# A hybrid encoder layer with 32 experts: token rows fetched as half rows to 128 partitions, and each expert's tokens dealt to slots four apart

## The reference

```python
grp_logits = xt @ w_grp + b_grp                      # 4 groups
g_sel = argmax(grp_logits);  p_g = softmax(grp_logits)[g_sel]
top_val, top_idx = top_k(e_logits[g_sel], 2)         # 2 of the 8 experts of that group
weights = p_g * softmax(top_val)
h = silu(xb @ w_e1[e]) * (xb @ w_e3[e])              # 1024 -> 512, for each token of expert e
y[token] += (h @ w_e2[e]) * weight                   # 512 -> 1024
```

## Time and profile before

| | us |
|---|---|
| median of 3 runs (1262.17 to 1263.38) | 1262.66 |
| the profiled execution, its own time | 1259.6 |
| its span, first to last instruction | 1257.9 |
| PE busy | 1103.4 (88%) |
| DVE busy | 434.3 (35%) |
| POOL busy | 384.7 (31%) |
| ACT busy | 356.3 (28%) |
| 96 weight loads of 2 MB, median issue to landing | 36.2 |
| DMA queue of the weights (q1), share of 16 engines | 51.8% |

### The profile page before, as it was taken

How to read it: one execution, slowest core, us unless ns; L and a number is a source line. 1 busy time by engine, 2 the same in 40 slices (tenths; PEclk the granted TensorE clock), 3 DMA queues, 4 the chain that set the end, 5 groups by cost and what they waited for, 6 DMA issues and landing times. The chain is left out here.

```text
span 1257.9 us, 20475 instructions
## 1 busy us (share of the span) xinstructions
PE 1103.4 (88%) x8243; PEld 841.1 (67%) x8243; DVE 434.3 (35%) x957; ACT 356.3 (28%) x749; POOL 384.7 (31%) x425
## 2 busy tenths in 40 slices
PE   5999899899999999998998978878888888777784
PEld 4998898899998878888996754444444444444342
DVE  6697633972111744432334432220101000000006
ACT  5547533452223645442334330000000000000000
POOL 4454468741223342333552011121221111111100
PEclk9999999989999989999998969989999999999998
DMA  7322336173325411116225939999999999999985
GB/s 126 88 81 68 77 88 168 45 196 98 93 53 180 142 34 51 52 43 214 80 72 174 429 122 407 404 406 400 404 406 408 405 406 415 404 402 404 405 373 226
DMA packets 149146, 284.58 MB, mean 226 GB/s; under 512 B 43988, under 2 KB 119348, under 8 KB 132688
## 3 DMA queue, kind: packets, MB, share of 16 engines
q1 hardware_dynamic: 93696, 244.94, 51.8%
q10 hardware_dynamic: 49632, 27.46, 8.1%
q0 software_dynamic: 5744, 11.15, 2.6%
HBM read 267.08 MB, written 24.31 MB: 232 GB/s over the span
## 5 line engine op out<-in xcount | busy, mean ns | idle before, releaser
L2528 PE MATMUL bank<-e_w,b_xT 128*64 128x256 f32 x2048 | 235.2, 387 | 37.0 <-DVE b_xT L2555 28.1
L489 PE MATMUL bank<-xhi,cv_w_hi 128*128 128x272 f32 x848 | 258.6, 305 | 8.4 <-PEq L133 2.6
L475 POOL TENSOR_TENSOR cv_w_lo<-cv_w_raw,cv_w_hi 128x1024 fp32r<-128x1024 f32 (+1 forms) x69 | 164.4, 2383 | 308.0 <-ACT cv_w_hi L468 291.5
L489 PE MATMUL bank<-xhi,cv_w_lo 128*128 128x272 f32 x848 | 249.3, 294 | 0.0
L489 PE MATMUL bank<-xlo,cv_w_hi 128*128 128x272 f32 x848 | 248.8, 293 | 0.0
L2528 PEld LDWEIGHTS bank<-e_w,b_xT 128*64 128x64 f32 x2048 | 145.9, 139 | 116.2 <-DVE b_xT L2555 33.5
L489 PEld LDWEIGHTS bank<-xhi,cv_w_hi 128*128 128x128 f32 x848 | 163.8, 193 | 17.1 <-issue 9.7
L489 PEld LDWEIGHTS bank<-xlo,cv_w_hi 128*128 128x128 f32 x848 | 164.6, 194 | 1.1
L489 PEld LDWEIGHTS bank<-xhi,cv_w_lo 128*128 128x128 f32 x848 | 164.1, 194 | 0.0
L2540 PE MATMUL bank<-e_w,b_hiddenT 128*64 128x512 f32 x512 | 124.9, 632 | 33.5 <-issue 18.3
L2496 POOL COPY b_target<-slot_target 128x1 int32 (+1 forms) x31 | 5.6, 181 | 358.4 <-ACT b_y L2550 358.4
(11 more groups left out here) (449 smaller groups left out, 1649.7 us busy)
## 6 DMA issues: line engine op xcount, KB each, us to landing
e_w<-in_w_e SPq DMA_DIRECT2D x96, 2048.0 KB, 36.2
cv_w_raw<-in_w_in ACTq DMA_DIRECT2D x34, 512.0 KB, 4.2
cv_w_raw<-in_w_in SPq DMA_DIRECT2D x18, 512.0 KB, 3.8
cv_w_raw<-in_w_br_b ACTq DMA_DIRECT2D x8, 512.0 KB, 4.2
o_raw<-in_w_out SPq DMA_DIRECT2D x16, 256.0 KB, 4.1
y_rows<-choice_rows SPq DMA_DIRECT2D x8, 512.0 KB, 6.8
g_values_gates<-g_z_stage ACTq DMA_DIRECT2D x12, 272.0 KB, 4.6
f_gates<-g_values_gates SPq DMA_DIRECT2D x2, 1088.0 KB, 8.7
```

The source lines that it names most:

```text
L475: self.k.nc.gpsimd.tensor_tensor(self.wlo[:, s, 0:nk, :], self.raw[:, s, 0:nk, :], self.whi[:, c % OPS, 0:nk, :].bitcast(F32), ALU.subtract)\
L489: last = self.k.nc.tensor.matmul(self.bank(c, h)[:, 0:HALF], w, x[:, d, cols], start=(d == 0 and n == 0), stop=(d == nk - 1 and n == 2))
L2528: last = nc.tensor.matmul(k.bank[bank][sl[a], 0:FH], xT[:, d, :], w[slot][:, d, FH * a:FH * a + FH], start=(d == 0), stop=(d == KD - 1))
```

## The change

Three things are changed, and small ones follow from them.

1. `b_rows` has 128 partitions of 512 floats: slot s has the first half of its token's row in partition s and the second half in partition 64+s. The gather reads half rows of 2 KB from a view of `token_rows` with two rows for a token; `token` numbers are doubled, and `k.half` adds 0 or 1 by partition half.
2. The turn takes the lower and the upper 64 partitions alternately, into banks 0 and 5; the gain is multiplied and copied in two instructions of 256 columns, and PE starts on the first four runs of channels after the first of them. `place_first` writes both halves of its product to one bank, and DVE adds them in one instruction.
3. Ranks are compared with `k.slots` in place of `k.iota`. It holds, in slot 4g+r, the number g+16r. So ranks 0 to 15 sit in slots 0, 4, 8, ..., ranks 16 to 31 in slots 1, 5, ..., and so on.

```diff
+SPREAD = SLOTS // 16
...
-    k.xg = k.over("b_rows", [SLOTS, RING, D], F32, "late", 3 * size)
+    k.xg = k.over("b_rows", [128, RING, D // 2], F32, "late", 3 * size)
+    k.halves = k.table.rearrange("t (two n) -> (t two) n", two=2)
...
+            g.iota(sN[:].rearrange("p (a g r) -> p a g r", a=2, r=SPREAD), pattern=[[0, 2], [1, SLOTS // SPREAD], [SLOTS // SPREAD, SPREAD]],
+                   base=0, channel_multiplier=0).then_inc(made, 1)
...
-                    last = V.tensor_scalar(r1[j][0:n, :], k.iota[0:n, :], k.rank[0:n, j, t:t + 1], None, ALU.is_equal)
+                    last = V.tensor_scalar(r1[j][0:n, :], k.slots[0:n, :], k.rank[0:n, j, t:t + 1], None, ALU.is_equal)
...
-            g.indirect_dma_start(out=xg[:, slot, :], out_offset=None, in_=k.table,
+            g.indirect_dma_start(out=xg[:, slot, :], out_offset=None, in_=k.halves,
...
-            nc.tensor.matmul(k.bank[0][:, 0:64], xg[:, slot, 0:128], k.ident[0:64, 0:64], start=True, stop=True)
-            for d in range(1, KD):
-                last = nc.tensor.transpose(k.bank[0][:, 64 * d:64 * d + 64], xg[:, slot, 128 * d:128 * d + 128],
-                                           k.ident[0:64, 0:64])
+            nc.tensor.matmul(X[0][:, 0:64], xg[lo, slot, 0:128], k.ident[lo, lo], start=True, stop=True)
+            nc.tensor.transpose(X[1][:, 0:64], xg[hi, slot, 0:128], k.ident[hi, hi])
+            for d in range(1, 4):
+                for a in range(2):
+                    last = nc.tensor.transpose(X[a][:, 64 * d:64 * d + 64], xg[sl[a], slot, 128 * d:128 * d + 128],
+                                               k.ident[sl[a], sl[a]])
...
-                nc.tensor.matmul(R[h][0:SLOTS, :], k.first_oh[:], k.xn[0:NS, 512 * h:512 * h + 512], start=True, stop=True)\
-                    .then_inc(placed, 1)
-            pe.wait_ge(joined, 2)
+                last = nc.tensor.matmul(R[sl[h], :], k.first_oh[:], k.xn[0:NS, 512 * h:512 * h + 512], start=True, stop=True)
+            last.then_inc(placed, 1)
+            pe.wait_ge(joined, 1)
...
-            nc.vector.tensor_tensor(xT[:], k.bank[0][:].rearrange("p (k s) -> p k s", k=KD),
-                                    k.gain[:].unsqueeze(2).broadcast_to([128, KD, SLOTS]), ALU.mult).then_inc(copied, 1)
+            for a in range(2):
+                f = slice(4 * a, 4 * a + 4)
+                nc.vector.tensor_tensor(xT[:, f], X[a][:, 0:4 * SLOTS].rearrange("p (k s) -> p k s", k=4),
+                                        k.gain[:, f].unsqueeze(2).broadcast_to([128, 4, SLOTS]), ALU.mult).then_inc(copied, 1)
...
-                    c(V.tensor_tensor(target[:, 0:n], target[:, 0:n], bank[:, n:2 * n], ALU.add))
-                    c(V.tensor_scalar(target[:, 0:n], target[:, 0:n], 2.0, half[:], ALU.mult, ALU.add))
-                    return V.tensor_copy(dst, target[:, 0:n])
+                    return V.scalar_tensor_tensor(out=dst, in0=target[:, 0:n], scalar=k.half[:, 1:2], in1=bank[:, n:2 * n],
+                                                  op0=ALU.add, op1=ALU.add)
...
-                for h in range(2):
-                    f = slice(512 * h, 512 * h + 512)
-                    v.wait_ge(placed, h + 1)
-                    V.tensor_tensor(xg[:, 0, f], xg[:, 0, f], R[h][0:SLOTS, :], ALU.add).then_inc(joined, 1)
+                v.wait_ge(placed, 1)
+                V.tensor_tensor(xg[:, 0, :], xg[:, 0, :], R[:], ALU.add).then_inc(joined, 1)
```

More of the change, by code:

```diff
@@ L2120, in expert_tensors @@
     k.lg, k.gm, k.em8, k.rank = keep("logits", 5, NL), keep("gmax", 5, 8), keep("emax", 5, 8), keep("rank", 2, 5)
-    k.oh, k.iota, k.token, k.total = keep("oh", 2, 5, NE), keep("iota", 2 * SLOTS), keep("token", 5), keep("total", NE)
+    k.oh, k.iota, k.token, k.total = keep("oh", 2, 5, NE), keep("iota", NE), keep("token", 5), keep("total", NE)
+    k.slots, k.half = keep("slots", 2 * SLOTS), keep("half", 2)
     k.xn, k.first_oh = keep("xn", D), k.sb("c_first_oh", [NS, SLOTS], F32, ctx)
-    k.first_idx, k.last_tabled = k.sb("c_first_idx", [SLOTS, 1], I32, ctx), sem("last_tabled")
+    k.first_idx, k.last_tabled = k.sb("c_first_idx", [128, 1], I32, ctx), sem("last_tabled")
     k.gain = k.sb("g_ffn_runs", [128, KD], F32, ctx)
@@ L2347, in _ @@
             V.memset(k.oh[:], 0.0)
+            for a in range(2):
+                for x in range(2):
+                    V.memset(k.half[64 * a:64 * a + 64, x:x + 1], 2.0 * (x + 1) * NT + a)
             V.memset(both[:], 0.0)
@@ L2352, in _ @@
                 V.tensor_tensor(k.x[0:n, t, 0:512], k.x[0:n, t, 0:512], k.bank[2 + t][0:n, :], ALU.add).then_inc(added0, 1)
-            v.wait_ge(made, 3)
-            V.tensor_copy(k.iota[:].rearrange("p (a s) -> p a s", a=2), iN[:])
+            v.wait_ge(made, 4)
+            V.tensor_copy(k.iota[:], iN[:])
+            V.tensor_copy(k.slots[:], sN[:])
             c(V.tensor_copy(k.token[:], token_i[:]))
@@ L2450, in expert_blocks @@
         T = lambda name, *dims: k.sb("m_" + name, [128] + list(dims), F32, ctx)
-        which, half, second, target = T("sums", 2 * NE), T("half", 1), T("second", NE), T("target", NE)
+        which, second, target = T("sums", 2 * NE), T("second", NE), T("target", NE)
         gd, e2, gs, wa = T("gdiff", 5, GROUPS), T("e2", 5), T("gsum", 5), T("wa", 5)
@@ L2526, in products @@
                 for d in range(KD):
+                    if bank == 1 and d == 4:
+                        pe.wait_ge(copied, 2 * b + 2)
                     for a in range(2):
@@ L2758, in beside @@
                     if b == 3:
-                        V.tensor_tensor(r1[:], k.iota[:].unsqueeze(1).broadcast_to([128, 10, 2 * SLOTS]),
+                        V.tensor_tensor(r1[:], k.slots[:].unsqueeze(1).broadcast_to([128, 10, 2 * SLOTS]),
                                         s_[:].unsqueeze(2).broadcast_to([128, 10, 2 * SLOTS]), ALU.is_equal)
@@ L2769, in beside @@
                         c(V.tensor_copy(k.eid[:], ejf[0:1, :]))
-                        c(V.tensor_copy(k.nmore[:], oi[0:1, 1, NE - 1:NE]))
                     if b == 5:
                         v.wait_ge(listed, 1)
-                        c(V.tensor_scalar(second[0:SLOTS, 0:MORE], M[0:SLOTS, 0:MORE], float(NT), None, ALU.add))
-                        c(V.tensor_tensor(k.idx[:, NE:], second[0:SLOTS, 0:MORE], M[0:SLOTS, MORE:2 * MORE], ALU.add))
-                        aim(M, MORE, k.dst[:, NE:]).then_inc(planned, 1)
+                        c(V.tensor_copy(which[:, 0:2 * MORE], M[:, 0:2 * MORE]))
+                        V.scalar_tensor_tensor(out=k.idx[:, NE:], in0=which[:, 0:MORE], scalar=k.half[:, 0:1],
+                                               in1=which[:, MORE:2 * MORE], op0=ALU.add, op1=ALU.add)
+                        c(aim(which, MORE, k.dst[:, NE:]))
+                        V.tensor_copy(k.nmore[:], oi[0:1, 1, NE - 1:NE]).then_inc(planned, 1)
                         c(V.tensor_tensor(ohw[:], k.oh[:, :, :, NE - 1], k.wt[:].rearrange("p t j -> p j t"), ALU.mult))
                         for t in range(5):
-                            V.tensor_scalar(last_oh[:, t, :], k.iota[:], k.rank[:, 0, t:t + 1], ohw[:, 0, t:t + 1],
+                            V.tensor_scalar(last_oh[:, t, :], k.slots[:], k.rank[:, 0, t:t + 1], ohw[:, 0, t:t + 1],
                                             ALU.is_equal, ALU.mult)
-                            c(V.tensor_scalar(other[:], k.iota[:], k.rank[:, 1, t:t + 1], ohw[:, 1, t:t + 1],
+                            c(V.tensor_scalar(other[:], k.slots[:], k.rank[:, 1, t:t + 1], ohw[:, 1, t:t + 1],
                                               ALU.is_equal, ALU.mult))
```

53 lines of the change are left out of this document (26 added, 27 removed).

## The result

The changed kernel takes 1230.93 us (median of 4, 1228.56 to 1238.46) against 1262.41 for the kernel before on the same chip: ratio 0.9749, 95% interval 0.972 to 0.9778. Measured again it was 1234.60 us (6 runs), ratio 0.9765 [0.9732, 0.9798]. The prediction was 1253.9 us, range 1249 to 1261: the sign was right, the size was not. 8.8 us were forecast, about 30 came.

The account below looks back on a forecast made before the run. The prediction took the expert stage's weight stream to bound the kernel. From the profiled 1259.6 us it took 6.8 (slots) and 2.0 (start), giving 1250.8 profiled and 1253.9 us for the median, range 1249 to 1261.

Parts of the forecast that it names:

- What bounds the kernel: Expert stage: the weight stream bounds it; shortening only PE's or DVE's work between 760 and 1217 us moves nothing.
- Slots four apart: End of the weight stream: dealing rows evenly over DMA engines shortens the uneven end, 6.8 us gained.
- D: Rival, weight stream: the deal does nothing because an engine's partitions already mix low and high slots; 1260.7 us, 0.20 with A.
- A: Rival, stream's end: uneven engines have another cause, only the start counts; 1260.7 us, chance 0.20 together with D.
- B: Rival, stream's end: late engines are slow ones that rows had spared, so the deal costs 5 us; 1265.7 us, chance 0.08.
- The start of block 0: Chain before the expert stage's first up product: three terms start the weight stream 2.0 us earlier, range 0 to 3.3.
- term (a): Block 0's start: the sample tokens' two matmuls overlap in two column halves, so DVE's add starts 1.1 us earlier.
- Term (b): Block 0's start: DVE's list loses two memsets and two of five target steps, together 0.6 us.
- term (c): Block 0's start: b_xT copied in two pieces lets PE start 0.27 us earlier.
- The gather in half rows: Gathers beside the weight stream: 128 indices instead of 64 cost nothing while landing stays under some 40 us.
- rival C: Weight stream: uneven engines cost rate too, so the change gives 6 us more; about 1248 us, chance 0.10.
- The end: Last scatter and read-back beside the stream's tail: both move forward with the stream's end, 0 of their own.

Follow-up runs that it names:

- e6: The kernel before with each gather's 64 rows of 4 KB going to every other one of 128 partitions: 1265.07 us, ratio 1.0009.
- e10: The kernel before with each gather's 64 rows of 4 KB going to partitions 32 to 95: 1262.32 us in one run.
- e1: The changed kernel with ranks put in slots 0, 1, 2, ... again, gathers still half rows to 128 partitions: 1238.67 us, ratio 0.9782.
- e2: The kernel before with only the slots four apart added, gathers still whole 4 KB rows to 64 partitions: 1261.84 us, ratio 0.9993.
- e3: The changed kernel with each gather of 128 half rows issued as two of 64, one per partition half: 1261.37 us, ratio 0.9979.
- e4: The kernel before with each gather naming 128 partitions, whole 4 KB rows filling only the lower 64: 1252.15 us, ratio 0.9911.
- e7: The changed kernel with each scatter of 128 half rows issued as two of 64 partitions, lower and upper half: 1237.08 us, ratio 0.98.

## Why the prediction was wrong, step by step

*What bounds the kernel*: right. The stream of weights did, and what moved this kernel's time moved it through the stream. That PE's work beside the stream moves nothing holds only while PE's block is short enough: at 15.2 us in e6 and e10 it did move the end.

*Slots four apart, 6.8 us*: inside the 4.5 to 9.0 us that I allowed, but only beside the gather over 128 partitions: 5.2 us by the stages of e1 and the changed kernel, 4 to 8 by the medians, and 3.1 in e2 without it. The sign that I named also came, an end of some 4 us instead of 16, but it took both changes: e1 (slots in order) and e2 and e3 (gathers into one half) each end over some 16 us. e1 and e4 show that unevenly filled partitions lengthen the end, so D is out, and A as the whole cause; e2 and e3 show that something else does too, which I did not have among the rivals. By B the deal would cost time, and in e1 taking it away costs 5.2 us, so B is out. The estimate of 744 KB rested on a rule for transfers over 128 partitions, while the gather before names 64.

*The start of block 0, 2.0 us*: right in size. The first up product starts 4.92 and 4.72 us behind the first matmul of the stage instead of 6.63, 1.7 and 1.9 us earlier. SP's first issue gained 1.45 us, 0.35 of it because the stage itself began earlier. The up product gave part back: more of it fell into the stretch at the low clock (0.50 granted until 750 us in both), and it took 9.98 us instead of 9.37 (0.71 granted over it against 0.76). The matmuls of the sample tokens took 1.99 us instead of 2.76, but they vary with the clock (1.09 to 1.99 us in the kernels with column halves, 1.91 to 2.76 in those with the order of before), so the 1.1 us of term (a) can't be read from one pair. At a granted clock of 1.00 they took 1.09 us in e7, with column halves, and 1.91 in e4, without, so 0.8 us at that clock. Term (b), from b_nothing's start to the list's end, measured 2.47 - 1.71 = 0.76 us against 0.6; term (c), the first b_xT, 0.61 - 0.34 = 0.27 us, as forecast.

*The gather in half rows, "It costs nothing"*: this is the step that failed. I looked at what issuing costs POOL (984 ns for 64 indices, 1061 for 128) and at the time to landing, and both did cost nothing. What I never priced was what the gather of before took from the weights beside it, because all its 64 partitions lie in one half: some 23.7 us. e3 takes the gain back by itself: stage 514.8 us against 488.0. That the kernel came out faster, as forecast, is to this extent luck: the larger part of the gain has a cause that the forecast did not hold.

*The rate*: I wrote that it stays at 405, and gave rival C, a gain of rate, 0.10 and 6 us, for the wrong reason (unevenness, which e1 excludes). The clue stood in the earlier trace rows: 405 GB/s from 1000 to 1194 us, 424 from 1194 to 1217 with the share at 1.00. I took this for engines that had less in their queues. POOL's timeline of the kernel before had the answer:

```profile
1179.70 0.99 POOL L2487 DMA_INDIRECT b_rows<-token_rows,b_index  x1 [0.54 <-issue]
1193.94 1.02 POOL L2499 DMA_INDIRECT choice_rows<-b_y,b_target  x1 [0.52 <-issue]
1208.90 0.99 POOL L2499 DMA_INDIRECT choice_rows<-b_y,b_target  x1 [0.52 <-issue]
```

The last gather is issued at 1179.70 us; scatters go on at 1193.94 and 1208.90. In the fast stretch weights and scatters run, and only gathers are missing. Stretches of 4 us around one gather, read in that trace, would have shown 333 beside 409 GB/s.

*The end, 0 of its own*: right within 0.5 us (23.1 and 23.5 us behind the start of the last read-back), the read-back taking 10.64 instead of 10.12 us.

## What to carry to other kernels

When a stream keeps all DMA engines busy and its rate differs between two stretches, list what other transfers run in the one and not in the other, and look at the rate in windows of a few us around one of them: a busy share of 1.01 hid 5% here. Let a gather that runs beside such a stream name partitions of both halves in one DMA: 0.14 MB per block into one half cost as much as 0.33 MB more of weights. And where a faster stream should pay, check that the consuming engine's pace per block leaves it room to catch up: at 15.2 us against 15.4 it did not, at 13.4 (the changed kernel) and 14.0 (e4) it did.

## What the runs showed of the hardware

- Rows gathered into partitions 0 to 63 or 64 to 127, by a DMA that names only these, pull the core's DMA rate down to 333 to 365 GB/s for some 4 us (403 to 407 on the mean); into 32 to 95, into every other one, or with 128 partitions named, they do not (427 from 1000 to 1160 us).
- Scatters that read from 64 partitions leave the rate at 426 to 428.
- Rows spread unevenly over partitions do not lower the rate while all engines have work (e1 and e4: 424 to 428); they lengthen the end, to some 16 us of falling share in e1 and 30 in e4.
- With rows dealt evenly the end is still some 16 us of falling share where a DMA of each block names 64 partitions (gathers in e2 and e3, scatters in e7), and some 4 us where none does.
- The time that an indirect DMA costs POOL hardly depends on its indices: 984 ns for 64, 1061 for 128. Two of 64 in place of one raised POOL's busy time from 50.77 to 64.20 us of 240 in e3.
